# Spreading a block's layer-norm rstd through DRAM and ScalarE instead of TensorE, in the output stage of a hybrid convolution layer

## What is computed

```python
def mixer_layer(x, ...):                                # x: (rows, 1024)
    proj = rms_norm(x, norm_g) @ w_in                   # 3584 columns, split in seven parts
    out_a = b_a * conv3(c_a * h_a) * silu(z_a)          # group A, 512 channels
    conv_b = causal_dwconv31(a_b * sigmoid(g_b)) + conv_b_bias       # group B, 512 channels
    s_b = silu(layer_norm(conv_b, ln_b_g, ln_b_b))      # mean and rstd over the 512 channels
    out_b = s_b * silu(z_b)
    return x + concat([out_a, out_b]) @ w_out           # followed by a final rms_norm
```

## Time and profile before

| what | us |
|---|---|
| median of 3 runs (1529.87 to 1531.67) | 1530.07 |
| the profiled execution, its own time | 1525.52 |
| its span in the trace | 1523.7 |
| output stage, from the last input tile to the end | about 1178 to 1523.7 |
| one block of the output stage (two pairs) | 40.66 |

### The profile page before, as it was taken

How to read it: one execution, slowest core, us unless ns; L and a number is a source line. 1 busy time by engine, 2 the same in 40 slices (tenths; PEclk the granted TensorE clock), 3 DMA queues, 4 the chain that set the end, 5 groups by cost and what they waited for, 6 DMA issues and landing times.

```text
span 1523.7 us, 19742 instructions
## 1 busy us (share of the span) xinstructions
PE 1509.9 (99%) x7184; PEld 1331.9 (87%) x7184; DVE 1287.2 (84%) x1295; ACT 586.8 (39%) x973; POOL 639.5 (42%) x563
## 2 busy tenths in 40 slices
PE   9999999999999999999999999999999999999998
PEld 8999999988888888888888888888898778888886
DVE  7699999998877998778788896798898788888875
ACT  5453443343333343323244322223343344444433
POOL 2886879012433331342423331116654544444441
PEclk9999999999999999999999999999999999999999
DMA  7898787699998889998889987776867754555541
GB/s 250 325 368 324 288 324 261 239 312 322 328 330 253 270 274 343 314 321 293 258 267 313 303 243 235 235 224 211 240 221 224 255 183 169 176 191 182 177 152 70
DMA packets 119825, 391.11 MB, mean 257 GB/s; under 512 B 17956, under 2 KB 23076, under 8 KB 116144
## 3 DMA queue, kind: packets, MB, share of 16 engines
q1 hardware_dynamic: 119728, 389.84, 75.4%
HBM read 281.31 MB, written 108.48 MB: 256 GB/s over the span
## 4 chain that ended last, share of the span: by engine, by line
PE 95%; DMA 2%; DVE 2%; issue 1%; ACT 0%; POOLq 0%; SPq 0%; POOL 0%; DVEq 0%; ACTq 0%
PE ps L2197 31%; PE ps L2199 31%; PE ps L2198 31%; DMA w_ring<-weight_forms 2%; PE ps L2324 0%; PE ps L2317 0%; PE ps L2402 0%; PE ps L2406 0%; DMA x_raw<-in_xT 0%; DVE conv_b L1994 0%; DVE w_ring L2017 0%; DVE xf_f L1752 0%; DVE ps L2010 0%; PE ps L2310 0%; PE ps L2208 0%
## 5 line engine op out<-in xcount | busy, mean ns | idle before, releaser
L1954 DVE SCALAR_TENSOR_TENSOR ps<-v,conv_b_taps,ps 128x920 f32<-128x920 f32 (+2 forms) x580 | 630.8, 1088 | 17.8
L2197 PE MATMUL ps<-xf,w_ring 128*128 128x460 f32 (+1 forms) x1624 | 603.0, 371 | 1.8 <-DMA w_ring<-weight_forms 0.9
L2199 PE MATMUL ps<-xf,w_ring 128*128 128x460 f32 (+1 forms) x1624 | 602.6, 371 | 0.0
L2198 PE MATMUL ps<-xf,w_ring 128*128 128x460 f32 (+1 forms) x1624 | 600.8, 370 | 0.0
L2197 PEld LDWEIGHTS ps<-xf,w_ring 128*128 128x128 f32 x1624 | 305.4, 188 | 36.4 <-issue 3.4
L2198 PEld LDWEIGHTS ps<-xf,w_ring 128*128 128x128 f32 x1624 | 305.4, 188 | 34.0
L2199 PEld LDWEIGHTS ps<-xf,w_ring 128*128 128x128 f32 x1624 | 304.9, 188 | 34.2
L1465 ACT ACTIVATE sets<-ps 128x460 f32<-128x460 f32 x168 | 92.7, 552 | 465.7 <-PE ps L2199 465.7
L1275 POOL TENSOR_TENSOR w_ring<-w_ring_f,w_ring 128x512 fp32r<-128x512 f32 x28 | 39.6, 1416 | 229.5 <-ACT w_ring L1495 229.5
L2197 PE MATMUL ps<-out_forms,w_ring 128*128 128x512 f32 x288 | 114.5, 398 | 2.5 <-DVE h_rows_odd L2126 2.0
L1226 POOL TENSOR_TENSOR sets<-sets 128x460 f32<-128x460 f32 x42 | 54.2, 1291 | 140.3 <-ACT sets L1465 140.3
(11 more groups left out here) (215 smaller groups left out, 2088.6 us busy)
## 6 DMA issues: line engine op xcount, KB each, us to landing
w_ring<-weight_forms SPq DMA_DIRECT2D x294, 512.0 KB, 5.6
x_raw<-in_xT SPq DMA_DIRECT2D x32, 460.0 KB, 7.1
weight_forms<-xf SPq DMA_DIRECT2D x7, 2048.0 KB, 13.1
weight_forms<-w_ring SPq DMA_DIRECT2D x7, 2048.0 KB, 12.2
out_weight_forms<-w_ring SPq DMA_DIRECT2D x28, 512.0 KB, 6.7
w_ring_f<-in_w_in SPq DMA_DIRECT2D x56, 256.0 KB, 3.6
xf_f<-in_w_in SPq DMA_DIRECT2D x26, 512.0 KB, 6.1
x_row<-in_x_prompt SPq DMA_DIRECT2D x24, 512.0 KB
```

The costliest lines, as they stand in the source:

```text
L1954: dve.scalar_tensor_tensor(dst, window, wb[:, j, k:k + 1], part, ALU.mult, ALU.add).then_inc(taps_done, 1)
L2197: pe.matmul(out, ahi, bhi, start=(start and x == 0), stop=False, skip_group_check=goes_on)
L2198: pe.matmul(out, ahi, blo, start=False, stop=False, skip_group_check=goes_on)
L2199: mm = pe.matmul(out, alo, bhi, start=False, stop=(stop and x == len(terms) - 1), skip_group_check=goes_on)
```

## The change

The rstd of blocks 2 to 8 is no longer spread by PE. SP writes `rstd_cols` to DRAM (2 KB) and reads it back broadcast to 128 partitions into `ta` (256 KB). ACT copies it into the PSUM bank, reordering the columns so that they stand in token order (`rows_of_rstd`). PE keeps the spread of blocks 0 and 1. For this the slots of blocks 2 to 8 move: `spread` (now ACT's copy and DVE's normalise) from 7 to 8, `silus` from 8 to 9, `gate` from 10 to 11. Block 1 goes the other way: all steps from `squares` on are one slot sooner. Its square sums on DVE now stand ahead of the low parts of P5 and P6. On ACT and POOL the column steps stand ahead of the row squares and the row rstd of the same slot. POOL's sums of the next block now also wait for the copy of the rstd.

```diff
-        FIRST_LN_SLOT = {"sums": 1, "sum_high": 3, "sum_low": 3, "mean": 4, "squares": 5, "square_sums": 6, "columns": 8,
-                         "spread": 10, "silus": 11, "gate": 12}
+        FIRST_LN_SLOT = {"sums": 1, "sum_high": 3, "sum_low": 3, "mean": 4, "squares": 4, "square_sums": 5, "columns": 7,
+                         "spread": 9, "silus": 10, "gate": 11}
         LN_SLOT = {"sums": -2, "sum_high": -2, "sum_low": -2, "mean": 1, "squares": 2, "square_sums": 3, "columns": 5,
-                   "spread": 7, "silus": 8, "gate": 10}
+                   "spread": 8, "silus": 9, "gate": 11}
...
+            def send_block_rstd(L):
+                sp.wait_ge(ln_cols_rstd, L + 1)
+                dst = rows_rstd_d[L].rearrange("(p c) -> p c", c=RT)
+                sp.dma_start(dst, rstd_cols[:, :]).then_inc(ln_rstd_out, 16)
+
+            def spread_block_rstd(L):
+                sp.wait_ge(ln_rstd_out, 16 * (L - 1))
+                sp.wait_ge(ln, ln_event(L, "squares"))
+                sp.dma_start(ta[:, 0, :], rows_rstd_d[L:L + 1, :].to_broadcast([P, OB])).then_inc(ln_rstd_in, 16)
...
+                    if t == 5 and L >= 1:
+                        send_block_rstd(L + 1)
+                        spread_block_rstd(L + 1)
                     if t == 6 and L + 1 <= OBLOCKS:
                         load_out_a(L + 1)
                     if t == 8 and L + 2 <= OBLOCKS:
                         load_cb(L + 2)
-                    if t == (13 if L == 0 else 11) and L + 2 <= OBLOCKS:
+                    if t == 12 and L + 2 <= OBLOCKS:
                         load_zb(L + 2)
...
                     pool.wait_ge(ln, ln_event(L - 1, "gated" if L == 1 else "squares"))
+                    need(pool, ln_var, L)
...
+                    if ln_due(m, i, "columns"):
+                        column_rstd(ln_due(m, i, "columns"))
                     if m and i == 0:
                         row_rstd(m - 1)
...
+            def rows_of_rstd(L):
+
+                c = col_tiles(L)
+                act.wait_ge(ln_rstd_in, 16 * (L - 1))
+                act.wait_ge(ln_cols_var, L + 1)
+                rows = ps[:, STAT_BANK, 0:ln_width(L)].rearrange("p (c t) -> p c t", c=c)
+                act.activation(rows, ta[:, 0, :].rearrange("p (t c) -> p c t", c=RT)[:, 0:c], ACT.Copy).then_inc(ln_var, 1)
...
+                    if (ln_due(m, i, "spread") or 0) > 1:
+                        rows_of_rstd(ln_due(m, i, "spread"))
                     if ln_due(m, i, "silus"):
                         silus(ln_due(m, i, "silus"))
...
                     if m + 1 < PAIRS and i == 5:
                         first_sums_of(m + 1)
-                        first_lows_of(m + 1)
                     if ln_due(m, i, "square_sums"):
                         square_sums(ln_due(m, i, "square_sums"))
+                    if m + 1 < PAIRS and i == 5:
+                        first_lows_of(m + 1)
...
-                    if ln_due(m, i, "spread"):
-                        column_spread(ln_due(m, i, "spread"))
+                    if ln_due(m, i, "spread") == 1:
+                        column_spread(1)
                     out_product(m, i)
```

More of the change, by code:

```diff
@@ L1349, in _ @@
                         sums(ln_due(m, i, "sums"))
-                    if ln_due(m, i, "columns"):
-                        column_rstd(ln_due(m, i, "columns"))
                     if i == 1:
@@ L1687, in _ @@
                         form_high_of(m, P4)
+                    if ln_due(m, i, "columns"):
+                        column_var(ln_due(m, i, "columns"))
                     if m and i == 0:
@@ L1692, in _ @@
                         sum_high(ln_due(m, i, "sum_high"))
-                    if ln_due(m, i, "squares") and i < 5:
+                    if ln_due(m, i, "squares"):
                         squares(ln_due(m, i, "squares"))
-                    if ln_due(m, i, "columns"):
-                        column_var(ln_due(m, i, "columns"))
                     if m + 1 < PAIRS and i == 4:
                         form_high_of(m + 1, P1)
+                    if (ln_due(m, i, "spread") or 0) > 1:
+                        rows_of_rstd(ln_due(m, i, "spread"))
                     if ln_due(m, i, "silus"):
@@ L1705, in _ @@
                         half_square(m, P2)
-                    if ln_due(m, i, "squares") and i >= 5:
-                        squares(ln_due(m, i, "squares"))
                     if i == 6:
@@ L2322, in column_spread @@
                 pe.wait_ge(ln_cols_rstd, L + 1)
-                for c in range(col_tiles(L)):
+                for c in range(RT):
                     mm = pe.matmul(ps[:, STAT_BANK, P * c:P * (c + 1)], rstd_cols[:, c:c + 1].to_broadcast([P, P]),
```

3 lines of the change are left out of this document (added).

## The result

| | before | after |
|---|---|---|
| median of 22 runs each, us | 1529.39 (1525.48 to 1532.26, and one of 3870.16) | 1531.36 (1529.01 to 1536.13) |
| the profiled execution, its own time | 1525.52 | 1533.67 |
| its span in the trace | 1523.7 | 1531.9 |
| output stage, from TensorE's first wait in slot 2 of block 0 to the end of the span | 339.3 | 342.6 |
| one steady block (blocks 2 to 6) | 40.66 | 41.43 to 41.47 |

The ratio after/before is 1.0023 with a 95% interval of 1.0014 to 1.0031: slower by 2 to 5 us. The launch of 3870.16 us is left out of the ratio; the two medians alone give 1.0013. The two profiled spans differ by 8.2 us, but 4.8 of them lie ahead of slot 2 of the output stage (1184.43 before, 1189.27 after), in code that the change does not touch.

A forecast was written before the change was run, and what follows sets the result against it. TensorE was taken to bound the kernel, VectorE next. Blocks 2 to 6 +4.2, block 7 -0.9, block 8 -0.2 and block 1 +0.7 gave +3.8 us on 1530.07: 1533.9, range 1523.5 to 1539.5.

The forecast's parts named there:

- What bounds the kernel: Output stage: TensorE, busy 99%, sets the time; its spread stands in the chain with 0.89 us a block, VectorE next.
- The new path for the rstd: Blocks 2 to 8: DMAs through DRAM and ScalarE's copy have the rows ready in time, with 1.4 us to spare.
- The normalise behind the first finish: Steady block, VectorE: the finish is blocked by GpSimd's low part of P4, so the normalise starts 4.2 us later.
- The chain to P5's high part: Steady block: normalise, silus, P1's form, gate and next block's sums make P5's high part 2.5 us later.
- The waits of one block: Steady block, TensorE: waits of 0.7 in slot 15 and 1.0 in slot 18, less 0.9 for the spread: +0.8 us.
- Block 1: Layer norm a slot sooner: its stall may go, but waits for later additions grow; +0.7 us, range -3.6 to +2.5.
- The stretch at the low clock: Block 1: granted clock 0.50 for 3.2 us behind a 2.0 us wait; full clock would gain 1.6 us.
- The port the other way round: Rival: VectorE wins the port at the finish, normalise 1.05 us sooner, a block gains 0.2; about 1527 us; chance 0.25.
- the late round trip: Rival: DMAs landing over 7.7 us after issue delay the normalise, 1 us per us in seven blocks; chance 0.08.
- The clock: Rival: waits bring the clock down once in each of five blocks, 1.6 us each, +8, 1542 us; chance 0.07.
- The DMAs: SP's queue: the load of out_a behind the two DMAs costs nothing unless the pair takes over 10 us.
- The full gain: Rival: margins of 2.7 and 1.7 us swallow all delays; -5.6 to -9.2 us, 1521 to 1524.5; chance 0.15.

The follow-up runs named there:

- kernel 6: The changed kernel with ScalarE's high part of P1 ahead of the silus and GpSimd's low part of P4 ahead of the row rstd; ratio to before 0.9974.
- kernel 8: As kernel 6, with block 1's layer norm in its old slots; median 1521.97 us beside 1529.05 for before, ratio 0.9954.
- kernel 3: The changed kernel with GpSimd's low part of P4 ahead of the row rstd from pair 1 on; ratio to before 1.0001.
- kernel 2: The changed kernel with ScalarE's high part of P1 ahead of the silus in odd pairs; ratio to before 0.9970.
- kernel 5: The kernel before with only the new DMAs added, their rows read by nobody; ratio to before 1.0002.
- kernel 1: The kernel before with spread, silus and gate of blocks 2 to 8 in the late slots, TensorE still spreading; ratio to before 1.0034.
- kernel 10: The changed kernel with only block 1's layer norm put back in its old slots; median 1530.37 us, ratio to before 1.0009.
- kernel 9: The kernel before, TensorE still spreading, with P1's high part ahead of the silus and P4's low part ahead of the row rstd; ratio 0.9991.

## Why the prediction came out as it did

The forecast was 1533.9 us, 3.8 above the kernel before; measured were 1531.36 beside 1529.39. The size of the effect is 2.0 us by the medians, 3.5 by the ratio, and 3.3 in the traces. Of the 2.5 us from 1531.36 to 1533.9, 1.8 are the smaller difference of the medians, and 0.7 is what the base that I carried over stood above the later median of the same kernel.

*What bounds the kernel.* Right, and kernels 6 and 8 show it best: with the waits away, a block is shorter by the full spread.

*The new path for the rstd.* The result was right, but by luck: each part was off, and the errors cancelled. Between the two issues lay 3.3 us in the block shown (2.0 to 3.3 over the seven), not 1.5. The broadcast landed in 4.5 (median of seven, 3.9 to 5.0), not 6.4. The copy took 1.10, not 0.61: I had named a stride of four as what could double it, and chose the lower end. From the columns (1329.57) to the rows (1338.26) it made 8.7 us, where I had 8.5. The normalise could have started 1.2 us sooner before the copy held it; I had 1.4. Kernel 3 is where this spare ran out.

*The normalise behind the first finish.* Right: blocked for 1.0, 5.8 us behind the start of slot 7 (1333.69 to 1339.48), and kernel 3 shows both the cause and what it costs, 0.9 us a block.

*The chain to P5's high part.* Right in order and size: 2.4 us later against 2.5.

*The waits of one block.* The total was right, the split was not. I had 0.7 in slot 15 and 1.0 in slot 18; measured were 0.61, 0.36 in slot 16, and 0.41, with 0.08 more for the matmul behind each. The step that failed is the one from P5 to P6 of the next pair: I left out that P6 waits for the addition of P1 ahead of it, which VectorE reached late as well. A wait that TensorE takes in slot 16 is one that it doesn't take in slot 18, so the sum stayed: 41.45 against 41.5, and +3.9 in blocks 2 to 6 against +4.2. Block 7 had 39.49 against 39.8; its predecessor had 40.40, so the -0.9 is right and the base of 40.66 was not that block's own.

*Block 1.* Right in size, +0.6 against +0.7, and partly by luck. Of its causes one was named (the normalise ahead of the addition of P6, 1.61 us); the waits at the mean and at P5 were not. The stretch at the low clock was wrong twice. I took it to follow from the wait of 2.0 us ahead of it; waits of 1.95 to 2.06 us on the way to block 2 have it behind them in the traces of before, 2 and 5, and not in those of 1, 3 and 10. And I priced it at 1.6 us, where it cost 0.3 to 0.5, since VectorE's additions set the pace there. Against a kernel before without that stretch, the new slots of block 1 cost 0.9 to 1.0 us.

*The rivals.* The port the other way round was priced at a block of 0.2 less and about 1527; kernel 3, which brings this about by order, had 0.1 less in a block. This is also the rival that the prediction means where it says what a form chain 1 to 2 us shorter would give; it names the third there, which is the late round trip. The clock stayed at 1.00 through the steady blocks' waits of 0.4 us. The DMAs were not late in the changed kernel, where out_a landed at most 12.9 us behind the column sums for a reader at 17.4, so the nothing at which I costed it holds. Kernels 2, 3 and 8 show that they are near it, at 0.4, 0.5 and 0.1 us in the blocks in which they came latest. The full gain was not impossible, only not reached by this order: kernel 8's stage is 7.9 us below before's, inside the 5.6 to 9.2 that the rival gave.

## What to carry to other kernels

Work taken off the bound engine is paid back if its replacement stands later in lists that other engines share: look for the order of the instructions behind it before judging the new path itself. Here one high part ahead of the silus and one low part ahead of a row rstd took 8.9 us off the stage of the changed kernel (342.6 to 333.7), which by itself had added 3.3. And where VectorE and GpSimd meet over SBUF, ask which of the two can be moved to the other side of the meeting; a transfer that waits for a GpSimd step moves with it. And before a stretch at the low clock is put down to the wait ahead of it, look for other traces with the same wait: here half of them had it.

## What the runs showed of the hardware

- **Who gets the port.** An instruction of VectorE with two SBUF inputs and one of GpSimd took turns in every meeting shown here, and whoever started first ran to its end: the finish 2.31 behind a low part that began 0.07 us sooner, 1.28 alone (kernels 1 and 3); in block 1 the gate 4.18 behind a sum, and in kernel 8 the gate 2.29 first and GpSimd's low part of the sum 2.94 behind it. The normalise, which has one input in PSUM, was never held: in kernel 9 it ran beside GpSimd for up to 1.8 us and took 2.28, and additions wholly beside a GpSimd instruction took 0.69. The Trainium skill (SBUF — State Buffer, section "SBUF: two separate sides") has the lock; the trace agrees with it. It runs on, as the prediction's chain has it: one late low part stretched the gate (3.35), then the sum (4.45), then VectorE's form sum (2.29).
- **A small round trip through DRAM** from one queue: after the issue of the 2 KB out it took 1.4 to 3.6 us until SyncE, waiting for it, issued the next (1.5 near the start of the program); the broadcast of 256 KB back took 3.9 to 5.0 in the changed kernel. From the first issue to the last landing the pair took 6.5 to 8.4 us in slot 5 of blocks 2 to 7, over all the kernels that have it.
- **A strided read on ScalarE**: 128x512 from SBUF to PSUM took 1.10 us with a stride of four elements in the input, where the row squares, of the same size and also from SBUF to PSUM, took 0.60, and the high part of P1 0.61.
- **The low clock comes and goes.** After a wait of TensorE of about 2 us on the way to block 2 the granted clock was 0.50 for 3.4 us in three traces (before, kernels 2 and 5) and stayed at 1.00 in three (kernels 1, 3 and 10). Before and kernels 1 and 10 have that wait at the same place, 1.95 to 1.97 us long.
